# Two-layer decoder step on one core: row-group gate products, Sqrt roots, a prompt tile first in layer 0's tail, query loads reordered

## The chip, the cores and the metric

The kernel runs on one core of a Trainium2 chip. Its time is the device time of one execution in microseconds (us), given as the median of several runs. All data are float32.

## What is computed

One inference step of a two-layer decoder for 512 new prompt rows and 8 request rows (520 rows of 1024 numbers). Layer 0 is an RWKV-7 time mix, layer 1 attention over keys and values made once between the layers. Each is followed by a norm, 16 experts with two chosen per row, and another norm. Of the reference, cut to what the change touches:

```python
# layer 0: end of the time mix
g = jax.nn.sigmoid(xg @ a_g1) @ a_g2               # inner size 160
out = ((yn + bonus) * g) @ a_w_o
# after each half layer
x = layer_norm(ALPHA * x + f, ln_g, ln_b)          # (x - mu) * rsqrt(var + LN_EPS) * g + b
# after layer 0
kv_new = einsum('btd,dgsnh->btgsnh', x, b_w_kv)    # 1024 -> 1536
# start of layer 1
q = x @ b_w_q                                      # 1024 -> 3072
```

## The kernel before

The 520 rows are five tiles: four of 128 prompt rows (tiles 0 to 3) and one of 8 request rows (tile 4). The program is a chain of blocks. In a block each engine (PE, DVE, ACT, POOL, and SP, which issues DMAs) has its own list of instructions, written out by hand, and waits on semaphores. Between blocks all engines meet at a barrier. So the order of work is the order of the lines in each engine's function, and nothing reorders it.

Weights come in chunks of 1 MB through a ring of 6 slots, and of 8 more (`ring_extra`) during the experts. `feed.upto(sp, used, stop, pool)` makes SP issue chunk loads up to number `stop`, into the slots of `pool` that have been held longest. Before each load SP waits on `slot_free`, which PE counts up when it has left a chunk (L227 is the issue). Behind such a wait, all that SP has left to do waits too. `take_chunk` makes PE wait until a chunk has landed.

**`time_mix_gate`** makes the gate for eight column tiles kt. PE's loop runs `centre` (L1202), `bonus_sum` (L1210), `variance` (L1218) and from kt = 4 `gate(kt-4)`; four gates are left for the end. A gate has an inner size of 160: for each half h of the rows a product with K = 128 (L1233) and one with K = 32 (L1234) that adds to the same bank. ACT takes logarithms (L1261) and exponentials (L1267), DVE finishes a tile at L1288, L1291 and L1295. L1295 waits for the gate's products.

**`output_norm`** runs after the time mix and after attention: PE multiplies tile after tile (L1358), DVE adds and takes statistics, `normalise` makes mean and variance (L1392, L1394), scales (L1398), waits for the root and finishes (L1401). ACT's `roots` makes 1/sqrt as exp(-0.5 ln v), two activations (L1417, L1419), each behind a load of its function table. PE then turns the tile (L1344).

**`expert_layer`** ends with a tail that gathers each row's two expert rows (POOL, L2129), adds them (DVE, L1695), norms (`statistics` L1695 to L1705, `roots` L1860 and L1862, `normalise` L1712) and stores. In layer 0 (`kv` given) the tail also makes keys and values: PE turns a normed tile (L2032), ACT keeps it (L1870), and PE multiplies it by six chunks of `b_w_kv` (L2064, 48 matmuls a tile). Requests go through `request_products` (L1310). ACT evacuates (L1874), PE turns keys (L2042), SP stores (L1784, L1797). The tiles go in the `order` (4, 0, 1, 2, 3): the requests first, then the prompt.

**`decode_and_prompt_attention`** begins with twelve query chunks (PE, L2408), which pass through the two `QUERY_SLOTS`. Two of them are issued before, behind the last chunk of layer 0's experts. In the block, SP loads the cached keys (L2245), waits until POOL's copies of the bias tables are stored (`bias.stored`), and then alternates: twelve small loads of bias tables (`bias.load`, L2186 and L2190), then one query chunk, eight times.

```python
                feed.upto(sp, 12, KV_END + 2, QUERY_SLOTS)
                sp.wait_ge(bias.stored, 48)
                for n in range(KVH):
                    for l in range(2):
                        bias.load(sp, landed[n // 2], n, l)
                        feed.upto(sp, 12, KV_END + 3 + 2 * n + l, QUERY_SLOTS)
```

## Time and profile before

| | |
|---|---|
| median of 3 runs | 1766.25 us (1763.91 to 1768.02) |
| profiled execution: time, span | 1764.17 us, 1762.3 us |
| PE busy, share of the span | 1562.2 us, 89% |
| DVE, ACT, POOL busy | 33%, 22%, 11% |
| mean granted PE clock | 0.941 of full speed |

The span is from the first to the last instruction. The stages by the trace, in us from the span's start: time mix to 437.8, gate 437.8 to 487.5, output norm to 562.0, layer 0's experts to 868, their tail to 998.8, attention to 1316, output norm to 1388.8, layer 1's experts to 1719, their tail to the end. A row of the timeline merges equal instructions: start, time from the first's start to the last's end, engine, line, operation, output and inputs, count, and in brackets the engine's idle time before it with what ended it. A float32 matmul of the program stands as two in the trace. SPq is SP's queue of DMA issues.

### The profile page before, as it was taken

What the parts mean: (1) busy time and instruction counts of PE and PEld (TensorE: products, weight loads), DVE (VectorE), ACT (ScalarE), POOL (GpSimd) and SP (SyncE); (2) the same over time, 40 slices, a digit from 0 to 9 for tenths busy, and PEclk for the clock granted to TensorE, in tenths of its full rate; (3) what the DMA queues carried; (4) which work ended last, traced back from release to release, by engine and by line L of the source; (5) the groups of instructions that cost most, each with busy time, mean ns of one, the idle gap of its engine ahead of it and who ended that gap; (6) DMA issues with size and microseconds to landing.
All of it is one profiled execution on the core that took longest, in us unless ns stands there. A gap on an engine that the chain in (4) does not pass through costs nothing. (4 is left out here: it accounts for less than half of the span.)

```text
span 1762.3 us, 46279 instructions
## 1 busy us (share of the span) xinstructions
PE 1562.2 (89%) x20468; PEld 1150.9 (65%) x20468; DVE 579.9 (33%) x1502; ACT 387.7 (22%) x928; POOL 194.3 (11%) x190
## 2 busy tenths in 40 slices
PE   7999999996997799999669879999999589999970
PEld 6878868875675455555458768887878445555540
DVE  5121545663544312121181100005654512121217
ACT  1023334331522011110122001115652201110113
POOL 1000025643300300000010000000000020000002
PEclk8999999998988799999979989999999799999995
DMA  9400001011424999999951375552120699999973
GB/s 288 166 32 25 1 4 35 28 34 37 158 72 167 342 376 384 379 383 382 355 157 48 97 108 123 119 106 87 37 74 0 260 336 384 378 380 380 380 268 145
DMA packets 218132, 331.09 MB, mean 188 GB/s; under 512 B 70456, under 2 KB 117344, under 8 KB 217936
## 3 DMA queue, kind: packets, MB, share of 16 engines
q1 hardware_dynamic: 193552, 285.13, 47.2%
q0 software_dynamic: 8208, 25.57, 5.4%
q10 hardware_dynamic: 16176, 17.43, 2.9%
q8 instruction: 164, 2.69, 0.6%
q14 instruction: 32, 0.26, 0.0%
HBM read 295.73 MB, written 32.39 MB: 186 GB/s over the span
## 5 line engine op out<-in xcount | busy, mean ns | idle before, releaser
L2408 PE MATMUL bank<-x_early,ring 128*128 128x256 f32 (+1 forms) x768 | 175.5, 390 | 15.1 <-DMA ring<-in_b_w_q 11.3
L1945 PE MATMUL bank<-ring_extra,xT 128*32 128x256 f32 x3264 | 180.5, 379 | 0.0
L2408 PEld LDWEIGHTS bank<-x_early,ring 128*128 128x128 f32 x768 | 148.0, 194 | 38.7 <-DMA ring<-in_b_w_q 11.5
L1945 PE MATMUL bank<-ring,xT 128*32 128x256 f32 x2880 | 162.9, 385 | 1.3 <-DVE xT L1643 1.3
L1945 PEld LDWEIGHTS bank<-ring_extra,xT 128*32 128x32 f32 x3264 | 104.4, 110 | 70.0 <-issue 2.7
L1945 PEld LDWEIGHTS bank<-ring,xT 128*32 128x32 f32 x2880 | 92.3, 111 | 66.4 <-issue 5.9
L1648 DVE TENSOR_TENSOR sg<-sg,bank 128x128 f32<-128x128 f32 x96 | 27.1, 282 | 297.9 <-ACT sg L1816 297.9
L1963 PE MATMUL bank<-ring_extra,hT 128*32 128x256 f32 x1920 | 107.7, 380 | 2.6 <-DVE hT L1656 1.8
L1816 ACT ACTIVATE sg<-bank 128x128 f32<-128x128 f32 x96 | 26.7, 278 | 357.5 <-PE bank L1945 357.5
L376 PE MATMUL bank<-mix,ring 128*128 128x260 f32 x448 | 100.5, 384 | 0.0
L376 PEld LDWEIGHTS bank<-mix,ring 128*128 128x128 f32 x448 | 84.5, 190 | 15.3 <-ACT k L558 2.4
L1963 PEld LDWEIGHTS bank<-ring_extra,hT 128*32 128x32 f32 x1920 | 62.9, 110 | 41.1 <-issue 3.9
L1824 ACT ACTIVATE yo<-bank 128x256 f32<-128x256 f32 x96 | 36.9, 385 | 165.9 <-PE bank L1963 165.9
L2092 POOL DMA_INDIRECT xe<-tokens,lists x28 | 25.5, 910 | 383.1 <-PE bank L1924 372.1
L1963 PE MATMUL bank<-ring,hT 128*32 128x256 f32 x1152 | 64.6, 380 | 0.0
L1656 DVE COPY hT<-bank 128x384 f32<-128x384 f32 x32 | 17.8, 557 | 140.1 <-PE bank L1934 140.1
L456 PE MATMUL bank<-mix,ring 128*128 128x260 f32 x256 | 57.0, 383 | 0.4 <-issue 0.4
L2570 ACT ACTIVATE qF<-bank 128x256 f32<-128x256 f32 x48 | 16.3, 396 | 184.2 <-PE bank L2408 184.2
L2064 PE MATMUL bank<-ring,x_early 128*128 128x256 f32 x256 | 56.7, 379 | 0.0
L1358 PE MATMUL bank<-ring,w 128*128 128x256 f32 x256 | 56.1, 380 | 0.0
L1358 PE MATMUL bank<-ring,x_early 128*128 128x256 f32 x256 | 56.1, 380 | 0.0
L456 PEld LDWEIGHTS bank<-mix,ring 128*128 128x128 f32 x256 | 48.6, 190 | 8.2 <-issue 0.8
(408 smaller groups left out, 2377.2 us busy)
## 6 DMA issues: line engine op xcount, KB each, us to landing
ring_extra<-in_moe_w_down SPq DMA_DIRECT2D x40, 1024.0 KB, 15.1
ring_extra<-in_moe_w_gate SPq DMA_DIRECT2D x70, 512.0 KB, 9.4
ring_extra<-in_moe_w_up SPq DMA_DIRECT2D x70, 512.0 KB, 13.2
ring<-in_moe_w_gate SPq DMA_DIRECT2D x62, 512.0 KB, 9.7
ring<-in_moe_w_up SPq DMA_DIRECT2D x62, 512.0 KB, 12.7
ring<-in_moe_w_down SPq DMA_DIRECT2D x26, 1024.0 KB, 15.0
ring<-in_a_w_rkv SPq DMA_DIRECT2D x12, 1024.0 KB, 7.1
expert_out<-yo ACTq DMA_DIRECT2D x128, 96.0 KB, 6.4
```

Of the source, the lines that this page charges most:

```text
L376: ins = pe.matmul(pair(job, h)[:, 0:HALF], w[:, kt, q * 128:(q + 1) * 128], mix[n][:, kt, half(h)], start=kt == 0, stop=kt == KT - 1)
L456: ins = pe.matmul(ps[2 * (mt % 2) + h][:, 0:HALF], w[:, kt, (mt % 2) * 128:(mt % 2 + 1) * 128], mix["v"][:, kt, half(h)], start=kt == 0, s ...
L1358: ins = pe.matmul(ps[2 * (t % 2) + q // 2][:, at:at + 256], z[:, kt, t * 128:(t + 1) * 128], w[q][:, kt, :], start=kt == 0, stop=kt == KT - 1)
L1648: dve.tensor_tensor(sg[:, u], sg[:, u], ps[u][:, 0:128], ALU.mult).then_inc(gd, 1)
L1656: dve.tensor_copy(hT[:, :, :], ps[7][:, 0:128 * SUBS].rearrange("p (u k) -> p u k", u=SUBS)).then_inc(hc, SUBS)
L1816: act.activation(sg[:, u], ps[u][:, 0:128], ACT.Sigmoid).then_inc(sd, 1)
L1824: act.activation(yo[e % 2][:, u], ps[3 + i % 2][:, 0:256], ACT.Copy).then_inc(yc, 1)
L1945: ins = pe.matmul(ps[u][32 * q:32 * q + 32, 0:256], xT[:, kt, 32 * u:32 * u + 32], gate_up(w, kt % 2, q), start=kt == 0, stop=kt == KT - 1)
L1963: ins = pe.matmul(ps[3 + i % 2][32 * r:32 * r + 32, 0:256], hT[:, u, 32 * k:32 * k + 32], w[k // 2][:, k % 2, 256 * r:256 * r + 256], star ...
L2064: ins = pe.matmul(ps[kv_banks[i % 2][b]][:, at:at + 256], x[:, kt, t * 128:(t + 1) * 128], w[q][:, kt, :], start=kt == 0, stop=kt == KT - 1)
L2092: pool.indirect_dma_start(out=xe[e % 2][0:CAP, :], out_offset=None, in_=core.tokens, in_offset=bass.IndirectOffsetOnAxis(ap=ids, axis=0)). ...
L2408: ins = pe.matmul(ps[2 * (job % 3) + h][:, 0:n], w[:, kt_, rr, :], z[:, kt_, lo:lo + n], start=kt_ == 0, stop=kt_ == 7)
```

## The change

It has five parts.

- Gate: the K = 32 pieces of `low_b` and `g2b` are loaded twice, onto partitions 0 to 31 and 32 to 63. PE does the two K = 128 products, then the two K = 32 products, half 0 on the first 32 rows and half 1 on the next 32. Each of these counts `gated` up.
- Output norms: DVE adds a `reciprocal`, ACT does one `Sqrt` in place of `Ln` and `Exp`. The roots of the experts' tail stay as they were.
- Layer 0's tail: the order is (0, 4, 1, 2, 3). PE multiplies prompt tile 0 first, the request products follow it, into banks 3, 4 and 7. DVE norms each tile right behind its statistics, and adds the requests up after all five. ACT's list follows.
- The first two query chunks are issued in the tail after the stores of the first two normed tiles, and no longer behind the experts' last chunks.
- Attention: the third query chunk is issued ahead of the wait for the bias tables, and each later one a place earlier.

```diff
-        g2a, g2b = core.sb(own, "g2a", [128, D])[:, :], core.sb(own, "g2b", [32, D])[:, :]
-        low_a, low_b = core.sb(own, "low_a", [128, ROWS])[:, :], core.sb(own, "low_b", [32, ROWS])[:, :]
+        g2a, g2b = core.sb(own, "g2a", [128, D])[:, :], core.sb(own, "g2b", [64, D])[:, :]
+        low_a, low_b = core.sb(own, "low_a", [128, ROWS])[:, :], core.sb(own, "low_b", [64, ROWS])[:, :]
...
                 sp.dma_start(low_a, low_dram[0:128]).then_inc(low_in, 16)
-                sp.dma_start(low_b, low_dram[128:160]).then_inc(low_in, 16)
                 sp.dma_start(g2a, io["a_g2"][0, 0:128]).then_inc(low_in, 16)
-                sp.dma_start(g2b, io["a_g2"][0, 128:160]).then_inc(low_in, 16)
+                for h in range(2):
+                    sp.dma_start(low_b[32 * h:32 * h + 32], low_dram[128:160]).then_inc(low_in, 16)
+                    sp.dma_start(g2b[32 * h:32 * h + 32], io["a_g2"][0, 128:160]).then_inc(low_in, 16)
...
-                        pe.wait_ge(low_in, 64)
+                        pe.wait_ge(low_in, 96)
...
+                    o = [ps[2 * gate_pair(kt) + h][:, 0:HALF] for h in range(2)]
                     for h in range(2):
-                        o = ps[2 * gate_pair(kt) + h][:, 0:HALF]
-                        pe.matmul(o, g2a[:, cols], low_a[:, half(h)], start=True, stop=False)
-                        ins = pe.matmul(o, g2b[:, cols], low_b[:, half(h)], start=False, stop=True)
-                    ins.then_inc(gated, 1)
+                        pe.matmul(o[h], g2a[:, cols], low_a[:, half(h)], start=True, stop=False)
+                    for h in range(2):
+                        own_rows = slice(32 * h, 32 * h + 32)
+                        pe.matmul(o[h], g2b[own_rows, cols], low_b[own_rows, half(h)], start=False, stop=True).then_inc(gated, 1)
...
-                    dve.wait_ge(gated, kt + 1)
+                    dve.wait_ge(gated, 2 * kt + 2)
...
-                    dve.wait_ge(ag, 2 * i + 1)
+                    dve.wait_ge(ag, 3 * i + 1)
                     dve.tensor_scalar(mv[0:n, t, 3:4], mv[0:n, t, 1:2], LN_EPS, None, ALU.add).then_inc(ag, 1)
+                    dve.wait_ge(ag, 3 * i + 2)
+                    dve.reciprocal(mv[0:n, t, 3:4], mv[0:n, t, 3:4]).then_inc(ag, 1)
...
-                    dve.wait_ge(root, 2 * i + 2)
+                    dve.wait_ge(root, i + 1)
...
-                    act.wait_ge(ag, 2 * i + 2)
-                    act.activation(mv[0:n, t, 2:3], mv[0:n, t, 3:4], ACT.Ln).then_inc(root, 1)
-                    act.wait_ge(root, 2 * i + 1)
-                    act.activation(mv[0:n, t, 2:3], mv[0:n, t, 2:3], ACT.Exp, scale=-0.5).then_inc(root, 1)
+                    act.wait_ge(ag, 3 * i + 3)
+                    act.activation(mv[0:n, t, 2:3], mv[0:n, t, 3:4], ACT.Sqrt).then_inc(root, 1)
...
-        order = (4, 0, 1, 2, 3) if kv else range(TILES)
+        order = (0, 4, 1, 2, 3) if kv else range(TILES)
+        at_place = [order.index(t) for t in range(TILES)]
...
-                        r = keys_values[0][0:REQ, 512 * h:512 * h + 512]
-                        dve.tensor_copy(r, ps[h][0:REQ, :]).then_inc(req_added, 1)
+                        r = keys_values[1][0:REQ, 512 * h:512 * h + 512]
+                        dve.tensor_copy(r, ps[kv_banks[1][h]][0:REQ, :]).then_inc(req_added, 1)
...
-                for i in range(3):
-                    statistics(i)
-                    if i:
-                        normalise(i - 1)
                 if kv:
                     kF, v0 = kv
+                    for i in range(TILES):
+                        statistics(i)
+                        normalise(i)
+                    keep_keys(0, 0)
                     add_requests()
-                statistics(3)
-                normalise(2)
-                statistics(4)
-                normalise(3)
-                if kv:
-                    keep_keys(0, 1)
-                normalise(4)
-                if kv:
-                    for u, i in ((1, 2), (2, 3), (3, 0), (4, 4)):
+                    for u, i in ((1, 2), (2, 3), (3, 1), (4, 4)):
                         keep_keys(u, i)
+                else:
+                    statistics(0)
+                    for i in range(1, TILES):
+                        statistics(i)
+                        normalise(i - 1)
+                    normalise(TILES - 1)
...
                 feed.upto(sp, 6 * EXPERTS, next_stop, every)
-                if kv:
-                    feed.upto(sp, 6 * EXPERTS, next_stop + len(QUERY_SLOTS), QUERY_SLOTS)
...
                             count += 16
+                    if kv and i == 1:
+                        feed.upto(sp, 6 * EXPERTS, next_stop + len(QUERY_SLOTS), QUERY_SLOTS)
                     if kv and i:
                         t = order[i - 1]
-                        sp.wait_ge(ev if t < 4 else req_added, 3 * (i - 1) if t < 4 else 12)
+                        sp.wait_ge(ev if t < 4 else req_added, 3 * (t + 1) if t < 4 else 12)
...
-                def evacuate(i, b):
-                    act.wait_ge(mm, 3 * (i - 1) + b + 1)
-                    act.activation(keys_values[i][:, 512 * b:512 * b + 512], ps[kv_banks[i % 2][b]][:, :], ACT.Copy).then_inc(ev, 1)
+                def evacuate(f, b):
+                    act.wait_ge(mm, 3 * f + b + 1)
+                    act.activation(keys_values[at_place[f]][:, 512 * b:512 * b + 512], ps[kv_banks[f == 2][b]][:, :], ACT.Copy).then_inc(ev, 1)
 
                 if kv:
                     roots(0)
                     keep(0)
                     roots(1)
+                    evacuate(0, 0)
+                    roots(2)
+                    evacuate(0, 1)
                     keep(1)
-                    roots(2)
-                    for i in range(1, TILES):
-                        evacuate(i, 0)
-                        evacuate(i, 1)
-                        if i + 1 < TILES:
-                            keep(i + 1)
-                        evacuate(i, 2)
-                        if i + 2 < TILES:
-                            roots(i + 2)
+                    roots(3)
+                    evacuate(0, 2)
+                    keep(2)
+                    roots(4)
+                    for f in range(1, 4):
+                        evacuate(f, 0)
+                        evacuate(f, 1)
+                        if f < 3:
+                            keep(f + 2)
+                        evacuate(f, 2)
...
-                    pe.wait_ge(kept, 2)
-                    for q in range(6):
-                        request_products(pe, ps[q // 2], x, w[q], 256 * (q % 2)).then_inc(req, 1)
-                    turn_rows(1)
-                    for i in range(1, TILES):
-                        t = order[i]
+                    for f in range(4):
+                        i = at_place[f]
                         pe.wait_ge(kept, 2 * i + 2)
                         for q in range(6):
                             b = q // 2
-                            if q % 2 == 0 and i == 2:
+                            if q % 2 == 0 and f in (1, 3):
+                                pe.wait_ge(ev, 3 * (f // 2) + b + 1)
+                            if q % 2 == 0 and f == 2:
                                 pe.wait_ge(req_added, 4 * b + 4)
-                            if q % 2 == 0 and i > 2:
-                                pe.wait_ge(ev, 3 * (i - 3) + b + 1)
                             at = 256 * (q % 2)
                             for kt in range(KT):
-                                ins = pe.matmul(ps[kv_banks[i % 2][b]][:, at:at + 256], x[:, kt, t * 128:(t + 1) * 128], w[q][:, kt, :],
+                                ins = pe.matmul(ps[kv_banks[f == 2][b]][:, at:at + 256], x[:, kt, f * 128:(f + 1) * 128], w[q][:, kt, :],
                                                 start=kt == 0, stop=kt == KT - 1)
-                                if i == 4 and q and kt == 0:
+                                if f == 3 and q and kt == 0:
                                     ins.then_inc(core.slot_free, 1)
                             if q % 2:
                                 ins.then_inc(mm, 1)
...
-                            if q == 1 and i >= 2:
-                                pe.wait_ge(ev, 3 * (i - 1))
-                                if i > 2:
-                                    pe.wait_ge(kept, 2 * i + 2)
-                                turn_keys(i - 1)
-                            if q == 3 and i < 4:
-                                if i > 1:
-                                    pe.wait_ge(k_kept, 2 * (i - 1))
-                                turn_rows(i + 1)
-                            if q == 3 and i == 4:
+                            if q == 1 and f:
+                                pe.wait_ge(ev, 3 * f)
+                                turn_keys(at_place[f - 1])
+                            if q == 3 and f == 0:
+                                turn_rows(1)
+                            if q == 3 and f in (1, 2):
+                                pe.wait_ge(k_kept, 2 * f)
+                                turn_rows(f + 2)
+                            if q == 3 and f == 3:
                                 pe.wait_ge(req_added, 12)
                                 pe.wait_ge(k_kept, 6)
-                                turn_keys(0)
+                                turn_keys(1)
+                        if f == 0:
+                            pe.wait_ge(kept, 4)
+                            for q in range(6):
+                                request_products(pe, ps[kv_banks[1][q // 2]], x, w[q], 256 * (q % 2)).then_inc(req, 1)
+                                if q == 1:
+                                    turn_rows(2)
...
-                feed.upto(sp, 12, KV_END + 2, QUERY_SLOTS)
+                feed.upto(sp, 12, KV_END + 3, QUERY_SLOTS)
                 sp.wait_ge(bias.stored, 48)
                 for n in range(KVH):
                     for l in range(2):
                         bias.load(sp, landed[n // 2], n, l)
-                        feed.upto(sp, 12, KV_END + 3 + 2 * n + l, QUERY_SLOTS)
+                        feed.upto(sp, 12, KV_END + 4 + 2 * n + l, QUERY_SLOTS)
```

The next rows are instructions in each engine's order (line, operation, output and inputs, shape, count). In the rows of the change, lines are those of the changed file, which are up to six higher. On PE, the second gate of `time_mix_gate` before, with what stands around it:

```order
L1218 MATMUL bank<-kk,const 128x260 x2
L1233 MATMUL bank<-low_a,g2a 128x260
L1234 MATMUL bank<-low_b,g2b 128x260
L1233 MATMUL bank<-low_a,g2a 128x260
L1234 MATMUL bank<-low_b,g2b 128x260
L1202 MATMUL bank<-w,const 128x260 x2
```

and in the change:

```order
L1219 MATMUL bank<-kk,const 128x260 x2
L1234 MATMUL bank<-low_a,g2a 128x260 x2
L1237 MATMUL bank<-low_b,g2b 128x260 x2
L1203 MATMUL bank<-w,const 128x260 x2
L1211 MATMUL bank<-r,const 128x260 x2
```

The two K = 32 products have come together, on two groups of 32 rows. On PE, the start of keys and values in layer 0's tail before (L2032 turns a tile, L1310 is a request product, L2064 a prompt product):

```order
L2032 MATMUL bank<-const,rows_home 128x8 x8
L1310 MATMUL bank<-ring_extra,x_early 8x256 x16
L1310 MATMUL bank<-ring,x_early 8x256 x32
L2032 MATMUL bank<-const,rows_home 128x128 x8
L2064 MATMUL bank<-ring_extra,x_early 128x256 x16
L2064 MATMUL bank<-ring,x_early 128x256 x16
L2032 MATMUL bank<-const,rows_home 128x128 x8
L2064 MATMUL bank<-ring,x_early 128x256 x16
L2064 MATMUL bank<-ring_extra,x_early 128x256 x16
L2042 MATMUL bank<-const,ring_extra 128x128 x6
```

and in the change, where L2037, L1312 and L2065 are these lines:

```order
L2037 MATMUL bank<-const,rows_home 128x128 x8
L2065 MATMUL bank<-ring_extra,x_early 128x256 x16
L2065 MATMUL bank<-ring,x_early 128x256 x16
L2037 MATMUL bank<-const,rows_home 128x8 x8
L2065 MATMUL bank<-ring,x_early 128x256 x16
L1312 MATMUL bank<-ring_extra,x_early 8x256 x16
L2037 MATMUL bank<-const,rows_home 128x128 x8
L1312 MATMUL bank<-ring,x_early 8x256 x32
L2065 MATMUL bank<-ring_extra,x_early 128x256 x16
L2047 MATMUL bank<-const,ring_extra 128x128 x6
```

The 48 request products have moved behind the first tile's 48, and the turns of tiles 4 and 1 into the middle. On SP, the start of the attention block before, from the cached keys on:

```order
L2245 DMA ring<-in_cache_kv_g 128x8x256 x2
L2245 DMA ring<-in_cache_kv_g 32x8x256
L2186 DMA near<-bias_copies_281 64x1x256 x4
L2190 DMA far<-bias_copies_282 64x1x32
L2190 DMA far<-bias_copies_283 64x1x32
L2190 DMA far<-bias_copies_282 64x1x64
L2190 DMA far<-bias_copies_283 64x1x64
L2190 DMA far<-bias_copies_282 64x1x96
L2190 DMA far<-bias_copies_283 64x1x96
L2190 DMA far<-bias_copies_282 64x1x128
L2190 DMA far<-bias_copies_283 64x1x128
L227 DMA ring<-in_b_w_q 128x8x64 x4
```

and in the change:

```order
L2251 DMA ring<-in_cache_kv_g 128x8x256 x2
L2251 DMA ring<-in_cache_kv_g 32x8x256
L227 DMA ring<-in_b_w_q 128x8x64 x4
L2192 DMA near<-bias_copies_281 64x1x256 x4
L2196 DMA far<-bias_copies_282 64x1x32
L2196 DMA far<-bias_copies_283 64x1x32
```

The first query chunk in this block (four DMAs) has moved from behind twelve bias loads and the wait ahead of them to a place in front of both.

## Rows read from the trace of the kernel before

**Rows 1.** Windows: length; busy us of PE, PEld, DVE, ACT, POOL; clock, DMA share, GB/s.

```profile
868.00:998.80 130.80, 98.40 (x550) 82.87 (x550) 46.14 (x66) 26.44 (x42) 11.01 (x10) 0.90 0.34 113
998.80:1316.00 317.20, 301.28 (x2867) 253.86 (x2870) 85.20 (x423) 91.48 (x266) 6.10 (x9) 0.97 0.43 97
```

**Rows 2.** Timeline, PE, one steady gate (start, duration, engine, line).

```profile
465.53 0.70 PE L1233 MATMUL bank<-low_a,g2a 128*128 128x260 f32 x2
466.16 0.70 PE L1234 MATMUL bank<-low_b,g2b 32*128 32x260 f32 x2
...
467.77 1.04 PE L1210 MATMUL bank<-r,const 128*128 128x260 f32 x4
...
468.65 1.04 PE L1218 MATMUL bank<-kk,const 128*128 128x260 f32 x4
```

**Rows 3.** Timeline, first wait and end of the gate block, PE and DVE.

```profile
459.10 0.70 PE L1233 MATMUL bank<-low_a,g2a 128*128 128x260 f32 x2 [0.48 <-DVE w L1295]
...
478.37 0.70 PE L1233 MATMUL bank<-low_a,g2a 128*128 128x260 f32 x2 [0.28 <-DVE w L1295]
...
483.54 0.76 DVE L1291 SCALAR_TENSOR_TENSOR a<-a,vecs,v 128x520 f32<-128x520 f32 x1
...
486.54 0.76 DVE L1295 TENSOR_TENSOR w<-bank,a 128x260 f32<-128x260 f32 x2 [2.23 <-PE bank L1234]
```

**Rows 4.** Timeline, PE, scores on two row halves in attention.

```profile
1199.80 0.70 PE L2344 MATMUL bank<-kF,qF 64*128 64x256 f32 x4
...
1200.34 0.63 PE L2346 MATMUL bank<-kF,qF 64*128 64x64 f32 x8
```

**Rows 5.** Timeline, DVE, last tile of the output norms; a reciprocal in attention.

```profile
554.11 1.27 DVE L1398 SCALAR_TENSOR_TENSOR rows<-rows,mv,gain 128x1024 f32<-128x1024 f32 x1
...
557.37 1.28 DVE L1401 SCALAR_TENSOR_TENSOR rows_home<-rows,mv,shift 128x1024 f32<-128x1024 f32 x1 [1.99 <-ACT mv L1419]
...
1384.16 1.28 DVE L1401 SCALAR_TENSOR_TENSOR rows_again<-rows_again,mv,shift 128x1024 f32<-128x1024 f32 x1 [2.00 <-ACT mv L1419]
...
1200.21 0.16 DVE L2478 RECIPROCAL m<-m 128x2 f32<-128x2 f32 x1
```

**Rows 6.** Timeline, layer 0's tail, all engines.

```profile
882.67 2.58 DVE L1695 SCALAR_TENSOR_TENSOR rows_home<-ring_extra,weights,rows_home 8x1024 f32<-8x1024 f32 x2 [21.19 <-DMA ring_extra<-expert_out,slots]
...
888.09 2.59 DVE L1695 SCALAR_TENSOR_TENSOR rows_home<-ring_extra,weights,rows_home 128x1024 f32<-128x1024 f32 x2
...
888.52 0.20 ACT L1862 ACTIVATE mv<-mv 8x1 f32<-8x1 f32 x1
...
899.63 3.71 PE L1310 MATMUL bank<-ring,x_early 128*8 128x256 f32 x64
...
905.10 7.17 PE L2064 MATMUL bank<-ring_extra,x_early 128*128 128x256 f32 x32 [0.74 <-ACT x_early L1870]
...
993.54 0.60 ACT L1874 ACTIVATE ring_extra<-bank 128x512 f32<-128x512 f32 x1 [6.97 <-PE bank L2064]
```

**Rows 7.** Timeline, start of attention: PE, then SP.

```profile
1017.96 7.18 PE L2408 MATMUL bank<-x_early,ring 128*128 128x256 f32 x32
...
1025.41 7.18 PE L2408 MATMUL bank<-x_early,ring 128*128 128x256 f32 x32
...
1044.30 10.06 PE L2408 MATMUL bank<-x_early,ring 128*128 128x256 f32 x32 [11.27 <-DMA ring<-in_b_w_q]
...
1028.99 2.50 SPq L2186 DMA_DIRECT2D near<-bias_copies  x4
...
1036.67 3.18 SPq L227 DMA_DIRECT2D ring<-in_b_w_q  x4
```

**Rows 8.** Windows of the start of attention.

```profile
1018.00:1029.00 11.00, 11.00 (x55) 9.60 (x54) 1.38 (x2) 1.21 (x6) 0.00 (x0) 1.00 0.87 85
...
1036.60:1044.30 7.70, 0.00 (x0) 0.00 (x0) 0.00 (x0) 0.00 (x0) 0.00 (x0) 0.50 0.94 179
1044.30:1050.00 5.70, 5.70 (x14) 4.55 (x15) 0.00 (x0) 0.00 (x0) 0.00 (x0) 0.50 0.17 34
```

6 lines of the change are left out of this document (3 added, 3 removed).

## The prediction

> **What bounds the kernel now.** I read the page first: the tensor engine (PE) is busy for 89% of the span and no other engine is near that, so time can only be won where PE stands still or works at less than its rate. Then the windows by stage. Two stages touched by the change have much open PE time: layer 0's tail has 98.4 us of work in 130.8, and attention leaves 15.9 us open at a mean clock of 0.97 [rows 1]. Then the timeline of each place, to see which wait ends last there. Four places matter. In the steady part of the gate block PE runs without a stop, and the spacing of its products is the limit [rows 2]; at the block's end DVE waits for PE [rows 3]. At the end of each output norm DVE waits for ACT's root [rows 5]. In layer 0's tail PE waits for the first normed tile and then works through to the end [rows 6]. At the start of attention PE waits 11.27 us for a query chunk [rows 7]. The rest of the program is not touched.
>
> **Gate.** The pairs of half-products start 0.63 us apart (465.53, 466.16), where four halves without a change of shape take 0.88, 0.44 a pair (467.77, 468.65) [rows 2]. So each change between K = 128 and K = 32 costs 0.19. A gate has four such changes, the change leaves two: 0.38 less. The K = 32 pair now lies on two row groups. The nearest row is the score products of attention, which alternate between two groups of 64 rows: four halves of 256 columns take 0.54 instead of 0.88 (1199.80 to 1200.34) [rows 4], 0.34 less. Together 0.72 a gate. The first gate's gain is lost, since the second waits for DVE at 459.10 in any case [rows 3]; the next three give 2.2 us, as ACT and DVE follow PE there. Four gates are left at the end. PE begins the last two at 478.37, after a wait for DVE, and DVE gets the last product at 486.54. With 2.2 us less before, and two gates of 0.72, twice that at the half clock in which they run, PE would be through at about 481.8. DVE has its own work up to 484.30 (483.54 + 0.76), less 2.2 is 482.1, so DVE takes over as the bound and the block ends 4.4 us earlier. If the row groups do not run side by side, 0.38 a gate is left: 1.1 before and about 1.1 in the last two, 2.2 in all. I take 4.4, since the rows of the scores show the overlap in this very program. Nothing speaks for a loss, because the number of products is the same. The ends are 0 and 4.4. The two more small loads on SP stand before chunks that are needed 48 us later: nothing.
>
> The Trainium skill (TensorE: Matmul & The Clock Gate, "Part 3: Packing small matmuls — row/col tiling") says that matmuls on different row groups start within some 4 ns of each other and run concurrently. By it the K = 32 pair would save the full 0.44, the three gates 2.5 and the term would be 4.7. The scores agree in kind and fall short in size.
>
> **Output norms.** The last tile's scaling starts at 554.11 and ends at 555.38, but the finishing step waits until 557.37 for the root, which needs two activations and two table loads. A reciprocal takes 0.16, with a gap of 0.04, and moves the scaling to 555.58; one Sqrt of the same size as Ln, with its table in place, is done meanwhile. So the last step starts at 555.6, 1.77 us earlier, and the next tail shows the same wait (2.00 at 1384.16) [rows 5]. Twice 1.77 is 3.5 us, all on the path, as PE's last turn and the barrier stand behind it. The earlier tiles gain nothing: PE's products cover them. Ends: 0 if ACT is late for another reason, and 5.3 if PE's shorter rest also spares it the half clock in its last turns (some 0.9 each). The table loads that now come before the next Exp stand in waits of ACT. In the experts' tails the roots are as before: nothing.
>
> **Layer 0's tail.** Before, DVE gets tile 4's rows at 882.67, its root is there at 888.72 (888.52 + 0.20), and PE's first prompt product starts at 905.10, behind the request products and a turn; ACT copies the last result at 994.14 (993.54 + 0.60). That is 89.0 us of PE work without a stop [rows 6]. In the change tile 0's rows come first. I take 883.1 for them, an estimate next to tile 4's landing. The ends are 882.67 and 888.09, when tile 0's sum began before without a wait. From there 6.05 to the root (as 882.67 to 888.72), 1.28 for the finishing step as in rows 5, and 1.8 for turn and copy (the request products end at 903.34, the prompt product starts at 905.10): the first product at about 892.3, 12.8 us earlier. Behind it come the same 89.0, and what formerly stood ahead of them: 96 halves of request products at the rate of 3.71 for 64, 5.6 us; a turn of tile 4, at most 1.0; and the half clock, which now falls on full products. The nearest row for that is PE's start after a wait in attention: 32 halves take 10.06 instead of 7.18, 2.9 us more [rows 7], of which 5.7 us are at clock 0.50 [rows 8]. 892.3 + 89.0 + 5.6 + 1.0 + 2.9 = 990.8 against 994.1: 3.3 us less. No other wait appears: tile 4's norm (some 7 us of DVE) is through before PE has done four of tile 0's six chunks, and so on by one tile; the request sums stand behind all norms on DVE but are wanted only one tile later, by the third prompt tile. The query chunks (formerly behind the experts) are now issued near 898 and wanted after 990; what is behind them on SP is stores. I count them at nothing, and nothing for what the gathers gain from the emptier queue. The ends are 1.7 slower (rows at 888.1) and 4.7 faster (a cold start at half that price).
>
> **Start of attention.** SP waits for the bias tables until 1028.99, loads one set (7.7 us), and only then issues the third query chunk, at 1036.67. PE has been idle since 1033 and goes on at 1044.30, 7.6 after the issue [rows 7]. In the change the chunk is issued when its slot comes free, at 1018, as PE begins the second chunk, and is there by 1033. That removes the wait of 11.27 us and the 2.9 us at half clock: 14.2. What is late next is the fourth chunk. It is now issued where the third was, at 1036.67, to land at 1044.3, and PE wants it at 1033 + 2 x 7.45 = 1047.8 (7.45 from job to job, 1017.96 to 1025.41) [rows 7]. That leaves 3.5 us. But the third chunk now travels beside the stores of the bias tables, which hold the DMA engines at a share of 0.87 from 1018 to 1029. The chunk itself, with most of a set of bias loads, took 0.94 of 7.7 us, 7.2 us of engine time [rows 8]; I take 5 for it alone, and let the tables be that much later. Then the fourth chunk lands at 1049.3, and PE waits 1.5. The term is 14.2 - 1.5 = 12.7. The ends: no delay, 14.2; the tables held up by 11 us, the whole stretch in which they share, a wait of 7.5 and the half clock again, 10.4, which leaves 3.8. From the fifth chunk on SP needs 7.7 + 3.2 = 10.9 us a round against PE's 14.9, and catches up.
>
> **Sum.** 4.4 + 3.5 + 3.3 + 12.7 = 23.9 us. The profiled execution took 1764.17 us, so it would take 1740.3. The median of the runs is 2.1 higher, and I put the median after at 1742.4.
>
> **Rivals.** (1) The wait moves from the third chunk to the fourth, because the tables are stored far later. For it: the DMA share of 0.87 leaves no room. Against it: the fourth chunk has 3.5 us in hand. Attention gives 3.8, in all 15.0: 1751.3 us. The Trainium skill (DMA: Bandwidth & Descriptors, "Queues, rings and completion order") says that a DMA engine goes round the queues packet by packet. The tables come from POOL's queue and the chunk from SP's, so by that rule both go on at about half speed, which is the delay of my forecast rather than the full one; no row here shows the two side by side. (2) Layer 0's tail gives nothing: tile 0's rows land as late as 888.1, or the cold start costs more. For it: PE has stood still since 867 and would start on full products. The tail is 1.7 slower, in all 18.9 faster: 1747.4. (3) The change does not do what it says in the gate, because the row groups run one after the other: 2.2 less, 1744.6. (4) Slower than before: bias loads and query chunks hinder each other so much that SP's round becomes the bound of the whole query projection. It decides from 14.9 us a round. To pay for the 23.9 us the round would have to last 17.9 over eight rounds; at 18.6, 29.6 us are lost and the result is 1772.0. Against it: the round is 10.9 now, with the same neighbours.
>
> **How the numbers follow.** Forecast 0.64, rival 1 0.13, rival 2 0.10, rival 3 0.10, rival 4 0.03. About 0.2% (3.5 us) is what a measurement can tell from no change. Only rival 4 ends there: a third of it within 0.2%, the rest slower. So 0.97 faster, 0.01 the same, 0.02 slower. For the range, the low end takes the norms at 5.3, the tail at 4.7 and attention at 14.2: 28.6 less, 1737.7, and 2 more for the spread of the runs, so 1736. The high end takes in rival 1 with 2 us for the runs: 1753. That leaves out rival 4 and corners where two terms fail together.
>
> **What would show it.** Gate: the K = 32 halves of a gate overlap, four within about 0.55 us, and DVE's last step no longer waits for PE. Norms: one table load, no wait of DVE before its last step. Tail: the first prompt product 9 us after tile 0's rows, at the half clock, and no PE wait until the end. Attention: no wait of 11 us at the fifth job, and at most 2 us at the seventh. The prediction is wrong if PE waits longer for the fourth chunk, if the first gather takes longer than the 8-row one, or if a wait for the request sums or for an ACT copy appears between the tail's products.

## The result, and the profile after

The changed kernel took 1742.68 us (median of 4 runs, 1738.52 to 1745.47), the kernel before on the same chip 1766.73 us: a ratio of 0.9864, with a 95% interval of 0.984 to 0.9888. A second series, beside experiment e12, gave 1741.11 us and 0.9882 (0.9861 to 0.9902). The forecast was 1742.4 us with 1736 to 1753. The profiled execution took 1743.93 us, span 1742.0 us (1764.17 and 1762.3 before), at a mean clock of 0.947 (0.941 before).

The page of the changed kernel, span and engines:

```profile
span 1742.0 us, 46263 instructions
...
PE 1556.5 (89%) x20468; PEld 1156.8 (66%) x20468; DVE 581.8 (33%) x1512; ACT 365.1 (21%) x902; POOL 192.9 (11%) x190
```

The mix of the engines is the same. The windows of layer 0's tail and of attention, cut at the same events as in [rows 1]:

```profile
861.30:991.40 130.10, 100.65 (x570) 84.36 (x562) 46.39 (x66) 26.83 (x43) 9.38 (x10) 0.90 0.38 120
991.40:1296.20 304.80, 298.39 (x2865) 251.81 (x2869) 85.14 (x423) 91.49 (x266) 6.12 (x9) 0.99 0.45 101
```

Attention is 12.4 us shorter (317.20 in [rows 1]), and PE's open time there has gone from 15.9 to 6.4 us.

**Gate.** PE's timeline of the changed kernel, a steady gate with its neighbours, then the end of the block on PE and DVE:

```profile
464.03 1.04 PE L1234 MATMUL bank<-low_a,g2a 128*128 128x260 f32 x4
465.00 0.71 PE L1237 MATMUL bank<-low_b,g2b 32*128 32x260 f32 x4
465.63 1.14 PE L1203 MATMUL bank<-w,const 128*128 128x260 f32 x4
...
476.39 1.85 PE L1234 MATMUL bank<-low_a,g2a 128*128 128x260 f32 x4 [1.89 <-DVE w L1297]
478.17 1.23 PE L1237 MATMUL bank<-low_b,g2b 32*128 32x260 f32 x4
...
482.75 0.76 DVE L1297 TENSOR_TENSOR w<-bank,a 128x260 f32<-128x260 f32 x2 [0.43 <-PE bank L1237]
```

And of the kernel before, the first product of the gate in [rows 2] and the first centring product behind it:

```profile
464.37 0.60 PE L1233 MATMUL bank<-low_a,g2a 128*128 128x260 f32 x2
...
466.79 1.14 PE L1202 MATMUL bank<-w,const 128*128 128x260 f32 x4
```

The four K = 32 halves last 0.71 us in all, and the next product starts 0.63 us after their first (465.00 to 465.63). The whole gate takes 1.60 us (464.03 to 465.63). Before it was 2.42 (464.37 to 466.79). At the end PE now waits 1.89 us for DVE, runs its last two gates at half clock, and DVE waits 0.43 us for the last product (2.23 in [rows 3]). The block, from its first product to DVE's last step, is 4.24 us shorter (44.42 instead of 48.66).

**Norm.** DVE's timeline for the last tile of output norm 1, to be held against [rows 5]:

```profile
548.58 0.21 DVE L1394 BATCH_NORM_AGGREGATE mv<-stats 128x2 f32<-128x12 f32 x1
...
549.01 0.16 DVE L1398 RECIPROCAL mv<-mv 128x1 f32<-128x1 f32 x1
549.10 1.26 DVE L1402 SCALAR_TENSOR_TENSOR rows<-rows,mv,gain 128x1024 f32<-128x1024 f32 x1
550.47 1.28 DVE L1405 SCALAR_TENSOR_TENSOR rows_home<-rows,mv,shift 128x1024 f32<-128x1024 f32 x1
```

and before, where the tile's statistics are joined:

```profile
553.79 0.21 DVE L1392 BATCH_NORM_AGGREGATE mv<-stats 128x2 f32<-128x12 f32 x1
```

The finishing step follows the scaling without a wait (1.99 before), and starts 1.89 us after the statistics are joined instead of 3.58.

**Tail.** The timeline of layer 0's tail in the changed kernel, POOL's first gather, DVE, PE and the last copy of ACT, against [rows 6]:

```profile
871.55 0.97 POOL L2135 DMA_INDIRECT ring_extra<-expert_out,slots  x1 [71.16 <-DMA expert_out<-yo]
...
879.00 2.60 DVE L1698 SCALAR_TENSOR_TENSOR rows_home<-ring_extra,weights,rows_home 128x1024 f32<-128x1024 f32 x2 [22.37 <-DMA ring_extra<-expert_out,slots]
...
886.49 1.97 PE L2037 MATMUL bank<-const,rows_home 128*128 128x128 f32 x8 [24.21 <-DVE rows_home L1715]
889.23 9.06 PE L2065 MATMUL bank<-ring_extra,x_early 128*128 128x256 f32 x32 [0.78 <-ACT x_early L1871]
...
986.11 0.60 ACT L1875 ACTIVATE ring_extra<-bank 128x512 f32<-128x512 f32 x1 [6.97 <-PE bank L2065]
```

and the first gather of the kernel before:

```profile
876.42 0.87 POOL L2129 DMA_INDIRECT ring_extra<-expert_out,slots  x1 [71.18 <-DMA expert_out<-yo]
```

From the first gather to the start of ACT's last copy it is 114.56 us; it was 117.12.

**Attention.** PE's timeline, then SP's, against [rows 7]:

```profile
1018.04 7.18 PE L2414 MATMUL bank<-x_early,ring 128*128 128x256 f32 x32
...
1027.47 7.28 PE L2414 MATMUL bank<-x_early,ring 128*128 128x256 f32 x32 [1.82 <-DMA ring<-in_b_w_q]
...
1011.21 11.34 SPq L227 DMA_DIRECT2D ring<-in_b_w_q  x4
1022.59 3.08 SPq L2192 DMA_DIRECT2D near<-bias_copies  x4
...
1031.33 3.06 SPq L227 DMA_DIRECT2D ring<-in_b_w_q  x4
```

The wait of 11.27 us is 1.82 now. It is still the third chunk that PE waits for; the fourth, issued at 1031.33, comes in time. SP needed 11.34 us to issue the four DMAs of the third chunk, where it takes 3.06 for the fourth and took 3.18 before. The DMA queues of the changed kernel (packets, MB, share of 16 engines; q1 is SP's queue, q0 POOL's with the bias copies) show where the chunk was, first from 1011 to 1020, then from 1020 to 1027.5:

```profile
DMA packets 229, 0.83 MB, mean 93 GB/s; under 512 B 32, under 2 KB 32, under 8 KB 229
...
q0 software_dynamic: 229, 0.83, 95.4%
...
q1 hardware_dynamic: 4556, 1.32, 95.1%
q0 software_dynamic: 38, 0.07, 8.5%
```

For the first 9 us no packet of the chunk moves. The first one starts at 1020.59, 9.4 us after the first issue, and the last copy lands at 1021.75. The copies themselves take as long as before: at most 16.0 us from POOL's issue to landing, 15.8 before.

### The profile page after: what moved, and what is told of

Read it like the earlier page. It is cut to its first block and busy times, and to the rows that moved or that the text cites. A ratio compares the mean times of both kernels' runs of the same rounds, so it can differ in the third digit from the quotient of the medians.

```text
span 1742.0 us, 46263 instructions
## 1 busy us (share of the span) xinstructions
PE 1556.5 (89%) x20468; PEld 1156.8 (66%) x20468; DVE 581.8 (33%) x1512; ACT 365.1 (21%) x902; POOL 192.9 (11%) x190
## 5 line engine op out<-in xcount | busy, mean ns | idle before, releaser
L1950 PE MATMUL bank<-ring,xT 128*32 128x256 f32 x2880 | 166.9, 387 | 3.5 <-issue 2.0
L1950 PEld LDWEIGHTS bank<-ring,xT 128*32 128x32 f32 x2880 | 97.8, 112 | 66.9 <-issue 11.7
L2065 PE MATMUL bank<-ring,x_early 128*128 128x256 f32 x256 | 56.8, 380 | 0.0
L1360 PEld LDWEIGHTS bank<-ring,w 128*128 128x128 f32 x256 | 48.3, 190 | 6.9 <-issue 0.4
```

What stands on the lines that cost most here:

```text
L1360: ins = pe.matmul(ps[2 * (t % 2) + q // 2][:, at:at + 256], z[:, kt, t * 128:(t + 1) * 128], w[q][:, kt, :], start=kt == 0, stop=kt == KT - 1)
L1950: ins = pe.matmul(ps[u][32 * q:32 * q + 32, 0:256], xT[:, kt, 32 * u:32 * u + 32], gate_up(w, kt % 2, q), start=kt == 0, stop=kt == KT - 1)
L2065: ins = pe.matmul(ps[kv_banks[f == 2][b]][:, at:at + 256], x[:, kt, f * 128:(f + 1) * 128], w[q][:, kt, :], start=kt == 0, stop=kt == KT - 1)
```

## The experiments

Beside the times of the kernels stand stage lengths from their profiles. They leave out most of what happened elsewhere in the run, and where two kernels do not differ in a stage, they show its scatter. The kernels ran on different chips, each beside the kernel before, so two of them are compared by what each is below the kernel before on its own chip. For the changed kernel this is 24.1 us in the first series and 21.3 in the second.

### The four parts, each alone

e1 is the kernel before with the gate's hunks of the change, e2 with those of the norms' roots, e3 with those of layer 0's tail (the new order and the later query loads, the third and fourth part of the change), e4 with these:

```diff
-                feed.upto(sp, 12, KV_END + 2, QUERY_SLOTS)
+                feed.upto(sp, 12, KV_END + 3, QUERY_SLOTS)
...
-                        feed.upto(sp, 12, KV_END + 3 + 2 * n + l, QUERY_SLOTS)
+                        feed.upto(sp, 12, KV_END + 4 + 2 * n + l, QUERY_SLOTS)
```

> The kernel before with the gate's part of the change alone (the 32 remaining rows of weights and activations twice, on row groups 0 and 1, the two 128-row products first). Theory of the prediction: 4.4 us less (three gates in a row at 0.72 each, the switches 0.38 each, DVE the bound at the end). What the trace of the changed kernel adds: output norm 1 starts 3.8 us earlier and the gate's first product 0.45 later, 4.2 in all; and of what layer 0 gains, its first expert's products lost 3 us (15.6 us for 12.6). If that loss belongs to any shift of the start, this kernel keeps only about 1 to 2 us of the 4.2; if it belongs to the shorter norm, it keeps all 4.2.

> The kernel before with reciprocal and Sqrt in the two output norms alone. Theory of the prediction: 1.77 us a norm, 3.5 in all. What the traces of both kernels say: from the norm's request products to the router 1.7 us in norm 1 and about 1.9 in norm 2 (the rest of the 3.1 of norm 1 came from the clock in the request products, which is the gate's doing). Rival: the first expert of each layer gives back what the norm gains (its products wait for their instructions while the DMA engines are full), then under 1 us in all and the third expert of layer 0 starts at the time it had before.

> The kernel before with layer 0's tail alone changed (row tile 0 first, the request rows second, the query chunks asked for after the first tile's rows are in). Theory of the prediction: 3.3 us less up to the last copy of ACT in the tail; the traces of both kernels give 2.6. Behind the tail the attention's start is as it was: its sixth product still waits for its chunk until 44.3 - 3.3 = 1041, since SP waits for its bias copies, whose end follows PE. If the wait stays at 11.3 us, the whole is 2.6 to 3.3 us faster; rival: the chunk's time hangs on DMA traffic, not on PE, then this kernel gains nothing (0 to 1 us).

> The kernel before with the third query chunk asked for ahead of the wait for the bias copies. Theory of the prediction: 11.3 us of PE's wait go, 2.9 of half clock behind it too, 1.5 come back as a wait for the fourth chunk: 12.7. The trace of the changed kernel shows instead 1.8 of a wait for the third chunk, whose four issues took SP 11.3 us, and 12.2 in all. If the parts are independent this kernel is 12.2 us faster, with a wait of 1 to 3 us for the third chunk; rival: without the tail's later query loads the chunk is asked for at another time and the wait is 0 or over 4.

Measured, against 1764.18 us for the kernel before on that chip:

| | us | ratio (95%) | less by the medians |
|---|---|---|---|
| e1 gate | 1760.13 | 0.9975 (0.996 to 0.9989) | 4.1 |
| e2 roots | 1759.73 | 0.997 (0.9953 to 0.9987) | 4.5 |
| e3 tail | 1759.74 | 0.9971 (0.9953 to 0.9988) | 4.4 |
| e4 attention | 1752.11 | 0.9925 (0.9889 to 0.9961) | 12.1 |

The four add up to 25.0 us, and the whole change gave 24.1 and 21.3 in its two series: nothing speaks against the parts being independent, but the four intervals together are too wide to show it. An interval of 2.5 us or more either way cannot size a term of 2 to 4 us, and the stages can. In e4 PE waits 1.4 us for the third chunk, whose issue takes SP 11.25 us, all as in the changed kernel. So that wait comes without the tail's later query loads.

The rival in e1 and e2, by which the first expert gives back what gate and norms gain, is out. The first expert of layer 0, from its first turn to the next expert's, took 17.7 us in the changed kernel and 14.7 in the one profile of the kernel before. But e3 and e4, which leave gate and norms alone, take 17.3 and 17.7, and the changed kernel run again takes 14.7. PE's timeline of the first expert, first in the changed kernel, with the stop after 45 products:

```profile
579.39 1.54 PE L1929 MATMUL bank<-const,xe 96*128 96x96 f32 x8 [6.89 <-DMA xe<-tokens,first_lists]
581.59 4.90 PE L1950 MATMUL bank<-ring,xT 128*32 128x256 f32 x45 [0.65 <-DVE xT L1646]
587.04 0.38 PE L1950 MATMUL bank<-ring,xT 128*32 128x256 f32 x1 [0.56 <-issue]
```

and in the same kernel run again (e11), without it:

```profile
577.80 1.54 PE L1929 MATMUL bank<-const,xe 96*128 96x96 f32 x8 [7.16 <-DMA xe<-tokens,first_lists]
579.99 12.58 PE L1950 MATMUL bank<-ring,xT 128*32 128x256 f32 x192 [0.65 <-DVE xT L1646]
```

The stop is there, in both layers, in nine of the twelve profiles in which nothing was done about it, in kernels with and without the change. It explains most of why the span fell by only 20.3 us where the medians fell by 24.1: the profile shown of before happened to be free of it in both layers, and its first two experts are 1.9 and 1.3 us shorter than those of the changed kernel's. The trace puts it down to PE's own issue, and its cause stays open.

### e5: what of the gate's gain is order, what is row groups

```diff
-                        own_rows = slice(32 * h, 32 * h + 32)
+                        own_rows = slice(0, 32)
```

> The gate alone as in e1_gate_alone (1760.1 us, gate to norm 45.7 us), but both 32-row halves use the copy on row group 0, so that only the order of the products is changed (a long, a long, a short, a short). Theory A (the prediction): two of four changes of the row count go, 0.38 a gate, and the side by side run of the two row groups gives 0.34 more; here the 0.34 goes: the four-part short group takes about 1.4 us instead of 0.71 while a pair of gate products takes some 2.3 us instead of 1.6 (2.64 before), and the block is 46.5 to 48 us. Theory B: the gain is all in the order; the short group still takes 0.7 and the block 45.7.

Measured: 1761.98 us, ratio 0.9982 (0.9967 to 0.9996). PE's timeline of e5, a steady gate:

```profile
462.72 1.04 PE L1234 MATMUL bank<-low_a,g2a 128*128 128x260 f32 x4
463.69 1.14 PE L1237 MATMUL bank<-low_b,g2b 32*128 32x260 f32 x4
464.76 1.14 PE L1203 MATMUL bank<-w,const 128*128 128x260 f32 x4
```

A gate takes 2.04 us here, 2.42 before, 1.60 in e1 and in the changed kernel. So the order gives 0.38 and the row groups 0.44. Theory B is out: the short group grows from 0.71 to 1.14. Theory A holds, with the short group at 1.14 instead of my 1.4; the block took 49.0, 1.0 us over the range given.

### e6: the query chunks asked for where they were

```diff
                 feed.upto(sp, 6 * EXPERTS, next_stop, every)
+                if kv:
+                    feed.upto(sp, 6 * EXPERTS, next_stop + len(QUERY_SLOTS), QUERY_SLOTS)
...
-                    if kv and i == 1:
-                        feed.upto(sp, 6 * EXPERTS, next_stop + len(QUERY_SLOTS), QUERY_SLOTS)
```

> The tail alone as in e3_tail_alone (1759.7 us), but the two query chunks are asked for where they were, ahead of the gather. Theory A (the place of the loads matters): the loads, 27.8 us of SP's issue in the kernel before, run beside the gather of the first full tile, the rows come later than 7.4 us after the first gather (up to 2 us more), and the kernel is up to 2 us slower than e3. Theory B (only the order of the tiles matters; the product of the first tile at 10 us after the rows, the request products in its shadow): the same time as e3 within 0.5 us.

Measured: 1763.22 us, ratio 0.9987 (0.997 to 1.0003); e3 had 0.9971. DVE's first sum in the tail, in e3 and in e6:

```profile
885.92 2.61 DVE L1696 SCALAR_TENSOR_TENSOR rows_home<-ring_extra,weights,rows_home 128x1024 f32<-128x1024 f32 x2 [22.31 <-DMA ring_extra<-expert_out,slots]
```

```profile
887.51 2.61 DVE L1696 SCALAR_TENSOR_TENSOR rows_home<-ring_extra,weights,rows_home 128x1024 f32<-128x1024 f32 x2 [23.75 <-issue]
```

With first gathers at 878.06 and 878.74 the rows come 7.86 us after the gather in e3 and 8.77 in e6. The eight kernels with the later loads have 6.8 to 8.5 us there, so e6 lies above them all, by 0.3 to 2.0: the loads seem to hold the gather up, but one profile cannot size it. PE's first product happened to take 9.32 us instead of 10.18, and from the gather to ACT's last copy e6 takes 116.14 us, e3 116.09. The median says 3.5 us, or 2.6 against the kernel before on each chip, with overlapping intervals, and the profile does not show more than 1.2 of it (the start of attention, up to its sixth product, takes 56.6 instead of 55.4). Inconclusive on the size; the sign points to theory A and is not shown.

### e7 and e9: are the bias copies what delays the third chunk?

e7 holds all three copies back and asks for the fourth chunk behind them:

```diff
                 sp.wait_ge(bias.stored, 48)
+                feed.upto(sp, 12, KV_END + 4, QUERY_SLOTS)
...
+                pool.wait_ge(mm, 3)
                 bias.store(pool, bias_kept)
```

> The changed kernel, with POOL's bias copies held back until PE has done the third query product, and the fourth chunk asked for ahead of the first bias load. Theory A: SP's issue of the third chunk took 11.3 us because the bias copies filled the DMA engines; without them it takes 3 to 4 us, PE's wait of 1.8 us before its fifth product goes, and nothing takes its place: 1.8 us faster, 1740.9. Theory B: the third chunk is late for another reason (its slot comes free at 1010 and the cache keys load beside it): its issue takes over 8 us and the wait stays, 1742.7. Rival C: the fourth chunk or the bias tables are late instead, a wait of over 2 us appears, 1743 or more.

Measured: 1746.05 us, ratio 0.9887 (0.9864 to 0.9911). PE's timeline of e7:

```profile
1026.03 7.18 PE L2416 MATMUL bank<-x_early,ring 128*128 128x256 f32 x32
...
1046.23 14.06 PE L2416 MATMUL bank<-x_early,ring 128*128 128x256 f32 x53 [5.57 <-DMA ring<-in_b_w_q]
```

The fifth product (1026.03) starts without a wait, and SP issued its four DMAs in 2.95 us (1011.75 to 1014.70), so theory A is right on the third chunk. But rival C came about: the fourth chunk is 5.57 us late, as this edit asks for it behind the wait for the copies (1035.98). In windows of this run from 1023 to 1035 the DMA engines are at a share of 0.92 to 0.96 while they move no more than 95 GB/s. The copies fill the engines with few bytes: in the changed kernel 229 of their packets, of 3.6 KB on average, hold the engines at 95.4% for 9 us.

e9 therefore splits the copies:

```diff
         for g, (lo, hi, _) in enumerate(self.parts):
+            if g == 1:
+                pool.wait_ge(products, 3)
...
-                feed.upto(sp, 12, KV_END + 3, QUERY_SLOTS)
+                feed.upto(sp, 12, KV_END + 4, QUERY_SLOTS)
                 sp.wait_ge(bias.stored, 48)
```

> The changed kernel, with the first of POOL's three bias copies where it was (1004.5) and the other two held back until PE has done the third query product (about 1018), and the fourth chunk asked for ahead of the wait for the copies. e7_bias_copies_later took the wait for the third chunk away and put 5.6 us for the fourth in its place, since the copies filled the DMA engines from 1018.6 to 1035 and SP asked for the fourth only behind them. Theory A (the chunks are late by what lies on the DMA engines when they are asked for, some 17 us of copies in all): the first copy is over near 1013, the third chunk's issue takes 4 to 6 us and no wait follows; the fourth chunk, asked for at 1025.6, meets only the rest of the copies and lands before 1040.5: the eight products from 1003 to 1063 run without a stop, 1.8 us faster than the changed kernel, 1740.9. Theory B (any load beside a copy waits for its end): one of the two waits stays, 1742.7 or more.

Measured: 1741.29 us, ratio 0.9879 (0.9857 to 0.9901). PE's timeline of e9, fifth product and on:

```profile
1026.51 7.18 PE L2416 MATMUL bank<-x_early,ring 128*128 128x256 f32 x32
...
1033.96 35.23 PE L2416 MATMUL bank<-x_early,ring 128*128 128x256 f32 x160
```

No chunk is late any more, and the start of attention up to the sixth product takes 41.5 us (43.6 in the changed kernel): theory A, 2.1 us. SP issues the third chunk's four DMAs in 4.25 us, and the chunk's first packet starts at 1014.43, 1.1 us before the one copy on the way lands. The time of the whole doesn't show the gain: 20.3 us below the kernel before, against the changed kernel's 24.1 and 21.3. The profile of e9 lost 3 us elsewhere, in a place the edit does not touch, to the clock. Windows of e9 in attention's scores:

```profile
1208.00:1212.00 4.00, 4.00 (x80) 3.24 (x76) 2.99 (x13) 3.13 (x9) 0.00 (x0) 1.00 1.07 357
1212.00:1216.00 4.00, 4.00 (x52) 3.49 (x48) 2.49 (x13) 1.56 (x5) 0.00 (x0) 0.83 1.07 389
1216.00:1220.00 4.00, 4.00 (x48) 3.53 (x47) 1.27 (x11) 1.88 (x6) 0.00 (x0) 0.50 0.20 74
```

### e8 and e10: what does the half clock cost?

```diff
                 if kv:
+                    pe.wait_ge(sums, TILES + 1)
+                    for _ in range(22):
+                        pe.matmul(ps[kv_banks[0][0]][:, 0:128], core.c("ident"), core.c("ident"), start=True, stop=True)
                     turn_rows(0)
```

> The changed kernel with 22 products of the identity (128x128, results unused) on PE in the layer 0 tail, between DVE's first sum and the first turn of the rows; nothing else is changed. It measures what the half clock costs there: turn 1.97 us and first prompt product 9.06 us for 32 products, against 1.0 and 7.1 at full clock. Theory A (the prediction's 2.9 us of half clock): the granted clock is up before the turn, and the kernel is 2.5 to 3 us faster, 1739.9. Theory B: 5.4 us of products do not bring the clock up before the turn: no change, or a part of it (0 to 1 us). If the products outlast the root, they delay the turn by what they overrun.

Measured: 1738.65 us, ratio 0.9847 (0.9823 to 0.9871). DVE's finishing step for the first tile in e8, then PE's timeline:

```profile
883.01 1.28 DVE L1715 SCALAR_TENSOR_TENSOR rows_home<-rows_home,mv,xe 128x1024 f32<-128x1024 f32 x1 [0.59 <-ACT mv L1863]
...
879.77 7.53 PE L2054 MATMUL bank<-const 128*128 128x128 f32 x44 [19.26 <-DVE rows_home L1698]
887.13 1.04 PE L2037 MATMUL bank<-const,rows_home 128*128 128x128 f32 x8
889.00 7.14 PE L2068 MATMUL bank<-ring_extra,x_early 128*128 128x256 f32 x32 [0.83 <-ACT x_early L1871]
```

Turn and first product run at full speed (1.04 and 7.14 us, against 1.97 and 9.06), 2.9 us less: theory A on the clock. But the 22 products last too long. The tile is normed at 884.29, and PE turns it only at 887.13, 2.8 us later, where the changed kernel turns it at once (886.43, 886.49). From DVE's first sum to ACT's last copy e8 takes 107.10 us and the changed kernel 107.11. So the profile shows no net gain in the tail. The time is 26.4 us below the kernel before (24.1 and 21.3 for the changed kernel), with overlapping intervals.

e10 puts the same 22 products into the wait for the first expert's rows:

```diff
                 pe.wait_ge(lists_made, 2)
+                for _ in range(22):
+                    pe.matmul(ps[0][:, 0:128], core.c("ident"), core.c("ident"), start=True, stop=True)
```

> The changed kernel with 22 products of the identity (results unused) on PE in the wait for the first expert's rows, in both layers: PE waits 6.9 and 6.7 us there and then works at half clock (turn 1.54 us; 45 products in 4.90, 0.109 each, against 0.055 at full clock), and stops for 2 to 3 us some 47 products on with nothing recorded but an instruction fetch. Theory A (half clock alone): the turn and the first products run at full clock and the kernel is about 3 us faster a layer, 1736.7. Theory B (the fetch sets the pace: the products stop until their instructions are there, whatever the clock): the stop grows by what the clock gives, and the first expert ends where it did, 1742.7. If the 22 products outlast the wait, the start is later by what they overrun, up to 1 us a layer.

Measured: 1740.65 us, ratio 0.988 (0.9853 to 0.9907). PE's timeline of e10, first and third expert:

```profile
581.56 10.57 PE L1952 MATMUL bank<-ring,xT 128*32 128x256 f32 x192 [0.85 <-DVE xT L1646]
592.06 0.88 PE L1931 MATMUL bank<-const,xe 96*128 96x96 f32 x8
...
605.86 0.88 PE L1931 MATMUL bank<-const,xe 96*128 96x96 f32 x8 [0.73 <-DMA xe<-tokens,lists]
...
1416.60 1.54 PE L1931 MATMUL bank<-const,xe 96*128 96x96 f32 x8 [2.85 <-DMA xe<-tokens,lists]
```

The first expert takes 12.2 us instead of 17.7 (16.7 in layer 1), and the stop is gone with the half clock, in both layers of e10 and of e12. Theory B is out. In layer 0 a wait of 0.73 us for the third expert's rows comes back. In layer 1 all of it comes back: the wait is 2.85 us, and behind it the third expert runs at half clock for its first 5 us and takes 20.0 us instead of 17.1. The time of the whole shows no gain: 20.9 us below the kernel before, against 24.1 and 21.3.

### e11 and e12: the changed kernel again, and all three additions together

e12 has e9's split and e10's products, and in the tail this in place of e8's loop:

```diff
-                    for _ in range(22):
+                    for _ in range(17):
```

> The changed kernel unaltered, as the base for e12_all_together on the same chip and as a second profile of it. 1742.7 us within the scatter. What the six profiles so far say of its stages: gate to norm 45.4 to 46.0 us with the clock down in the last two gates; first expert to third 30 to 31 us, with a stop of 2 to 3 us after some 47 products (Theory A: the stop is a property of the kernel, also of the one before, and only its one profile shown was spared it); last product of the layer 0 tail to the sixth query product 43.6 us, with 1.5 to 2 us of wait for the third chunk.

> The changed kernel with three additions at once: 17 products of the identity before the first turn of the layer 0 tail (22 overran by 1 us in e8_warm_tail), 22 in the wait for the first expert's rows in both layers (e10_warm_first_expert), and the bias copies split with the fourth chunk ahead of the wait for them (e9_bias_copies_split). Theory A: the gains are in stages apart and add: 2.9 (tail) + 3.2 and 2.9 (experts, of the 5.5 of the first expert some goes to a wait for the third expert's rows) + 2.1 (chunks) = 11 us less than the changed kernel, 1731.6. Theory B: the medians of the three runs alone (4.0, 2.0 and 1.4 less) are the better measure: 7.4 us, 1735.3. Theory C: a PE that is kept busy loses its clock elsewhere, as once in e9 (0.50 from 1216 to 1220 with PE busy): 1738 or more.

Measured: e11 1741.11 us, ratio 0.9882 (0.9861 to 0.9902); e12 1734.94 us, ratio 0.9852 (0.9831 to 0.9873), against 1762.43 for the kernel before. e12 is the fastest kernel of the study, 6.2 us below the changed one on the same chip by the medians, though the two intervals overlap. Of the three theories B (7.4 us below the changed kernel) is the nearest to the 6.2 measured, and A (11) is too much; the intervals do not rule out C. Against e11 its profile has the first two experts of layer 0 shorter by 2.3 us, the tail by 3.6, the start of attention by 1.9 and the first two experts of layer 1 by 0.5, 8.3 in all. Of the tail's 3.6, 1.0 is that e11's tail was the longest of its kind. With 17 products the turn comes at once (PE's timeline of e12):

```profile
879.20 5.61 PE L2056 MATMUL bank<-const 128*128 128x128 f32 x34 [18.52 <-DVE rows_home L1698]
884.92 1.09 PE L2039 MATMUL bank<-const,rows_home 128*128 128x128 f32 x8
```

and from DVE's first sum to ACT's last copy e12 takes 104.36 us, 2.8 less than the changed kernel's profile and 3.1 less than the mean of the seven kernels with the new order and without such products in the tail (106.8 to 108.2). The gate block with the request products behind it is 1.6 longer, which no edit touches.

## Why the prediction was right

Stage lengths from all profiles, in us. "As before" are the kernels that leave the stage alone, "changed" those that have its part as in the changed kernel; in the tail e10 is left out, whose third expert starts late (it takes 382.8).

| stage | as before | changed | less | predicted |
|---|---|---|---|---|
| gate's first product to the norm | 47.8 to 51.9, mean 49.9 (5) | 45.3 to 46.0, mean 45.6 (8) | 4.3 | 4.4 |
| norm 1, prompt products to router | 67.95 to 67.97 (6) | 65.8 to 66.7, mean 66.4 (8) | 1.6 | 1.77 |
| norm 2, the same | 67.84 to 67.85 (6) | 65.8 to 66.4, mean 66.1 (8) | 1.8 | 1.77 |
| third expert to attention (tail) | 383.6 to 384.2, mean 383.9 (5) | 381.2 to 382.9, mean 381.9 (5) | 2.0 | 3.3 |
| attention to its sixth product | 55.4 to 56.6, mean 55.8 (6) | 43.3 to 44.0, mean 43.6 (5) | 12.2 | 12.7 |

The sum is 21.9 us, against 23.9 forecast. The time of the whole came nearer to the forecast than the sum of the stages did, and one step of the largest term was wrong, so a part of the hit is luck.

**Gate.** The step "each change 0.19, two of four go, 0.38" was exact (e5). The overlap was put at 0.34 from the scores and is 0.44 (e1 against e5): a gate gives 0.82, not 0.72. The 0.34 was a reading of unlike rows: the 0.88 has no change of shape behind it and the 0.54 has one, while the gate's own pair has one both times (1.07 us from start to next start in e5, 0.63 on two row groups). Here the measurement is what the Trainium skill says (TensorE: Matmul & The Clock Gate, "Part 3: Packing small matmuls — row/col tiling"), by which the pair would save its full 0.44. For a product of this shape it was the better guide than the nearest row. What kept the term from the 4.7 that followed from it is the end of the block. I had DVE as the bound there. PE does wait 1.89 us for DVE, but behind that wait it runs at half clock and is last again by 0.43 us: without this the block would be 4.67 us shorter and not 4.24. So my sign that DVE's last step no longer waits for PE did not come. The size of the term also hangs on something I did not know. The unchanged block takes 47.8 us when its last gates run at full clock (e2, e4) and 51.9 when they run at half (e3, e6); the profile shown of before lies between. The gain is 2.2 us or 6.3, depending on the execution, and 4.3 on average.

**Norms.** Right, step by step. DVE's finishing step starts 1.89 us after the tile's statistics are joined (548.58 to 550.47); before it was 3.58. The optional 0.9 us for a last turn at a higher clock did not come in this profile, where it still takes 1.97 us. In the other seven kernels with this part it takes 1.09 to 1.71 us in norm 1, and the stage shows no clear gain for it (65.8 to 66.7 us, against 66.3 here).

**Tail.** The mechanism was right and the size 1.3 too high. In the profile shown it is 2.6, on average 2.0. The rows came 7.45 us after the first gather; I had assumed 6.7 (883.1 against 876.42). That was one of my signs of being wrong, a first gather longer than the 8-row one (6.25 before), and it did come, at a cost of 0.8 us. Turn and copy took longer: 10.23 us from the rows to the first product where I had 9.2, as the turn also runs at half clock (1.97 instead of 1.10). Later rows stood in my ends; the slower turn I had put at nothing. In return PE's work from there on was 1.0 us shorter than summed. The half clock itself I took at 2.9; the first product shows 1.6 to 3.0 in seven profiles (8.76 to 10.18 for 7.17), and e12 confirms the size, turn included, by taking it away: 2.8 to 3.1.

**Attention.** The sum came out right and its place wrong: a wait of 1.5 us that I had at the fourth chunk did not come, and one of 1.82 that I had not came at the third. That they are alike is luck. The step that failed is "I take 5 for it alone, and let the tables be that much later. Then the fourth chunk lands at 1049.3, and PE waits 1.5." It is the third chunk that was held up, and not the tables. The copies took 0.2 us longer at most (16.0 against 15.8 to landing). SP reached the first bias load 31.14 us after the start of attention (1022.59 from 991.45), and 30.10 before (1028.99 from 998.89): 1.0 us later, not 5, and that was its own slow issue, as the copies had landed at 1021.75. The chunk went from its first issue to PE's product in 16.3 us (1011.21 to 1027.47), and in 7.6 before. I had costed how long the DMA engines work for the chunk (7.2 us at most) and let it travel beside the copies. It did not travel beside them: for 9.4 of the 16.3 us none of its packets moved, and then it took 6.9. e4, e8, e10 and e11 show the same, with 9.4 to 9.6 us from the first issue to the first packet, which starts 1.0 to 1.3 us before the last copy lands. e7 and e9 show the cause: with the copies moved away the wait for the third chunk goes. Whether SP's slow issue (11.34 us) holds the packets back or is itself held up by the same thing stays open. That an issue can stall was in the trace of before: SP needed 27.26 us for the eight DMAs of the first two chunks, beside the gathers of the tail. In the rule of the Trainium skill (DMA: Bandwidth & Descriptors, "Queues, rings and completion order"), a DMA engine goes round the queues packet by packet, so both should go at about half speed. The trace does not agree: neither queue was at half speed, the copies went on as before and the chunk stood still. The measurement decides.

Of the rivals, (1), the wait moving to the fourth chunk, did not come with this change, but e7 made it happen with another order: 5.57 us. (2) and (3) are out: the tail is 1.5 us shorter in e3 than on average before and 2.0 in all (the table), and the row groups do run side by side (e5). (4) did not come: SP's round is 11.5 us in the changed kernel (from its issues at 1031.33 to those at 1042.81) against PE's 14.9.
